# State-space chunks: decays from differences of prefix sums that every partition reads from memory, in place of matrix products

## The reference, cut to what matters

```python
def ssd_chunked(xs, dt, A, Bm, Cm):
    ...
    xd = (xs * dt[..., None]).reshape(b, c, CHUNK_3, H, P)
    a = (dt * A).reshape(b, c, CHUNK_3, H).transpose(0, 3, 1, 2)
    a_cs = jnp.cumsum(a, axis=-1)
    L_intra = jnp.exp(segsum(a))
    scores = jnp.einsum('bclhn,bcshn->bhcls', Ch, Bh) * L_intra
    y_diag = jnp.einsum('bhcls,bcshp->bclhp', scores, xd)
    ...
```

## Time and profile before

| | us |
|---|---|
| median of three runs (3662.11 to 3667.56) | 3666.65 |
| the profiled execution, its own time | 3663.11 |
| its span in the profile | 3661.3 |
| TensorE busy, and its share of the span | 3538.3, 97% |
| VectorE busy | 2080.5, 57% |
| ScalarE busy | 935.3, 26% |
| GpSimd busy | 1093.3, 30% |
| mean granted TensorE clock, as a share of full speed | 0.988 |

### The profile page before, as it was taken

How to read it: one execution, slowest core, us unless ns; L and a number is a source line. 1 busy time by engine, 2 the same in 40 slices (tenths; PEclk the granted TensorE clock), 3 DMA queues, 4 the chain that set the end, 5 groups by cost and what they waited for, 6 DMA issues and landing times. The chain is left out here.

```text
span 3661.3 us, 46083 instructions
## 1 busy us (share of the span) xinstructions
PE 3538.3 (97%) x18166; PEld 2876.8 (79%) x18166; DVE 2080.5 (57%) x2838; ACT 935.3 (26%) x1662; POOL 1093.3 (30%) x1069
## 2 busy tenths in 40 slices
PE   7999999999999999999999999799999999999998
PEld 5777776688888888788888888588878878787776
DVE  6464557524233236699945555644535697753564
ACT  4444445300000004311111100411221123652132
POOL 2221121233333333233332233033332234024332
PEclk9999999999999999999999999999999999999999
DMA  2010010212212111122221121221293224432211
GB/s 100 24 30 30 24 35 13 75 58 62 70 57 74 57 57 58 35 98 86 86 81 70 41 81 65 91 87 41 87 181 86 82 78 131 145 103 75 73 54 64
DMA packets 139240, 260.19 MB, mean 71 GB/s; under 512 B 45632, under 2 KB 87616, under 8 KB 136000
## 3 DMA queue, kind: packets, MB, share of 16 engines
q1 hardware_dynamic: 73360, 156.78, 14.7%
q10 hardware_dynamic: 65712, 101.10, 8.1%
HBM read 209.35 MB, written 46.14 MB: 70 GB/s over the span
## 5 line engine op out<-in xcount | busy, mean ns | idle before, releaser
L650 PE MATMUL bank<-xh,wh 128*128 128x512 f32 x3024 | 1192.8, 394 | 30.1 <-DVE xl L2107 12.1
L653 PE MATMUL bank<-xl,wh 128*128 128x512 f32 x3024 | 1183.1, 391 | 0.0
L654 PE MATMUL bank<-xh,wl 128*128 128x512 f32 x3024 | 1181.9, 391 | 0.0
L609 POOL CAST wh<-raw 128x512 fp32r<-128x512 f32 x528 | 345.7, 655 | 2364.4 <-PE bank L654 2202.5
L611 POOL TENSOR_TENSOR wl<-raw,wh 128x512 fp32r<-128x512 f32 x528 | 733.9, 1390 | 42.3
L650 PEld LDWEIGHTS bank<-xh,wh 128*128 128x128 f32 x3024 | 569.4, 188 | 168.0 <-issue 18.7
L654 PEld LDWEIGHTS bank<-xh,wl 128*128 128x128 f32 x3024 | 569.5, 188 | 122.3 <-issue 0.7
L653 PEld LDWEIGHTS bank<-xl,wh 128*128 128x128 f32 x3024 | 570.0, 188 | 118.0 <-issue 1.3
L2407 DVE SCALAR_TENSOR_TENSOR bank<-apad,cols,bank 128x512 f32<-128x512 f32 x406 | 267.9, 751 | 0.0
L2145 DVE TENSOR_TENSOR h<-bank,h 128x512 f32<-128x512 f32 x240 | 165.6, 691 | 145.5 <-PE bank L654 144.8
L2276 DVE TENSOR_TENSOR gt<-sa,bank 128x512 f32<-128x512 f32 x44 | 30.3, 688 | 347.8 <-PE bank L654 347.8
(11 more groups left out here) (339 smaller groups left out, 4876.9 us busy)
## 6 DMA issues: line engine op xcount, KB each, us to landing
raw<-in_wstream SPq DMA_DIRECT2D x264, 512.0 KB, 3.5
spills<-spill ACTq DMA_DIRECT2D x38, 512.0 KB, 2.9
rawm<-in_mod_w ACTq DMA_DIRECT2D x12, 1024.0 KB, 4.9
gate_spill<-gates ACTq DMA_DIRECT2D x16, 512.0 KB, 2.6
tabs<-in_rope ACTq DMA_DIRECT2D x4, 2048.0 KB, 8.9
f<-spills SPq DMA_DIRECT2D x8, 1024.0 KB, 5.6
h<-in_x ACTq DMA_DIRECT2D x4, 1024.0 KB, 11.8
tabs<-gate_spill ACTq DMA_DIRECT2D x4, 1024.0 KB, 7.4
```

The source lines that it names most:

```text
L609: nc.gpsimd.tensor_copy(wh[:, slot, k], raw[:, slot, k]).then_inc(S("panel_high"), 1)
L650: mm = nc.tensor.matmul(o, lh, rh, start=start, stop=False, skip_group_check=shared)
L653: nc.tensor.matmul(o, lh, rl, start=False, stop=False, skip_group_check=shared)
L654: return nc.tensor.matmul(o, ll, rh, start=False, stop=stop, skip_group_check=shared)
```

## The change

The prefix sums that `dec_sum` leaves in bank 3 are copied, negated, into `dtmp` (step on the partitions, chunk and head along the free dimension). TensorE transposes `dtmp` once (`cs_turn`), between the halves of the first `z_last` tile. ScalarE copies the transpose out with the sign turned back, and writes it to memory as 128 rows of 128 steps, one row per chunk and head (`cs_rows`, 64 KB). For each chunk one DMA on SP's queue reads the chunk's 16 rows, 8 KB, into every one of the 128 partitions (`csb`, 1 MB in all). ScalarE then forms |prefix(t) - prefix(s)| in 16 instructions of 128x128 (`Abs` with `dtmp` as a bias per partition) and exp(-x) in place in four of 128x512. The products with `after` and the operand `mt` are gone, and `csb` takes the room of `mt`. VectorE multiplies with the masked scores group by group, and `ssd_intra` waits group by group. The wait of `ssd_inter` on the decays is dropped, and `ssd_turn_x` gains one on `xt_ready`.

In SP's program the DMA of `csb` for chunk c stands ahead of that of `f`. For c = 0 it waits for the stored rows and for `pc_ready`, for later chunks until ScalarE has read the chunk before out of `csb`, which has one buffer.

```diff
@@ sync: chunk loop
                 for c in range(CHUNKS):
+                    if c:
+                        sp.wait_ge(S("lt_spans"), 4 * c)
+                    else:
+                        sp.wait_ge(S("cs_stored"), 16)
+                        sp.wait_ge(S("pc_ready"), KT)
+                    sp.dma_start(csb[:, :, :].rearrange("p h t -> p (h t)"),
+                                 cs_rows.rearrange("(c h) t -> c (h t)", c=CHUNKS)[c:c + 1].broadcast_to(
+                                     [P, SSD_HEADS * P])).then_inc(S("csb_in"), 16)
                     for m in range(2 if c == 0 else 0):
                         sp.wait_ge(S(f"spilled{m}"), 16 * 19)
@@ tensor
+                def cs_turn():
+                    pe.wait_ge(S("cs_kept"), 1)
+                    nc.tensor.transpose(banks[2][:, 0:P], dtmp[:, :, :].rearrange("p c h -> p (c h)"), M["ident"]
+                                        ).then_inc(S("dec_sum"), 1)
...
                 for m in range(2):
-                    tile_x(units("z_last") + 2 * m, panels("z_last") + m, between=lambda: s5_outputs(6 + m))
+                    def within_z():
+                        if m == 0:
+                            cs_turn()
+                        s5_outputs(6 + m)
+
+                    tile_x(units("z_last") + 2 * m, panels("z_last") + m, between=within_z)
...
             def ssd_turn_x(c):
                 pe.wait_ge(S(f"f_in{c % 2}"), (c // 2 + 1) * 16)
+                if c:
+                    pe.wait_ge(S("xt_ready"), c)
...
-            def ssd_decays(c):
-                pe.wait_ge(S("mt_ready"), c + 1)
-                for q in range(4):
...
-                    nc.tensor.matmul(banks[seg_banks[q]][:, :], M["after"],
-                                     mt[:, 4 * q:4 * q + 4, :].rearrange("p h t -> p (h t)"),
-                                     start=True, stop=True).then_inc(S("seg_done"), 1)
...
             def ssd_intra(c):
-                pe.wait_ge(S("w_masked"), c + 1)
                 for hd in range(SSD_HEADS):
+                    if hd % 4 == 0:
+                        pe.wait_ge(S("w_masked"), 4 * c + hd // 4 + 1)
...
             def ssd_inter(c):
-                pe.wait_ge(S("lt_ready"), 4 * c + 4)
...
-                ssd_decays(0)
...
-                        ssd_decays(c + 1)
@@ scalar
                     if e == DT_SOFT:
                         softplus()
+                act.wait_ge(S("dec_sum"), 1)
+                A(dtmp[:, :, :].rearrange("p c h -> p (c h)"), banks[3][:, 0:P], ACT.Copy, scale=-1.0
+                  ).then_inc(S("cs_kept"), 1)
                 for m in range(2):
...
                     if m == 0:
-                        act.wait_ge(S("pc_ready"), KT)
-                        for part in range(2):
-                            ssd_steps(0, part)
                         y_store(6)
+                        act.wait_ge(S("dec_sum"), 2)
+                        A(cs_turned, banks[2][:, 0:P], ACT.Copy, scale=-1.0).then_inc(S("cs_kept"), 1)
+                        act.wait_ge(S("cs_kept"), 2)
+                        act.dma_start(cs_rows[:, :], cs_turned).then_inc(S("cs_stored"), 16)
                 load_functions(EXP_AND_LN)
-                act.wait_ge(S("dec_sum"), 1)
@@ ssd_exp
-                for q in range(4):
-                    act.wait_ge(S("seg_done"), 4 * c + q + 1)
-                    A(lt[:, 4 * q:4 * q + 4, :], banks[seg_banks[q]][:, :].rearrange("p (h t) -> p h t", t=P),
-                      ACT.Exp).then_inc(S("lt_ready"), 1)
+                act.wait_ge(S("csb_in"), 16 * c + 16)
+                for hd in range(SSD_HEADS):
+                    mm = A(lt[:, hd, :], csb[:, hd, :], ACT.Abs, bias=dtmp[:, c, hd:hd + 1])
+                    if hd % 4 == 3:
+                        mm.then_inc(S("lt_spans"), 1)
+                for g in range(SSD_GROUPS):
+                    act.wait_ge(S("lt_spans"), 4 * c + g + 1)
+                    A(lt[:, 4 * g:4 * g + 4, :], lt[:, 4 * g:4 * g + 4, :], ACT.Exp, scale=-1.0
+                      ).then_inc(S("lt_ready"), 1)
...
-                for part in range(2):
-                    ssd_steps(1, part)
...
-                    if c + 2 < CHUNKS:
-                        ssd_steps(c + 2, 0)
                     ssd_root(c)
-                    if c + 2 < CHUNKS:
-                        ssd_steps(c + 2, 1)
@@ vector: ssd_weights
-                dve.wait_ge(S("lt_ready"), 4 * c + 4)
                 dve.wait_ge(S("sm_ready"), c + 1)
-                l4 = lt[:, :, :].rearrange("p (g h) t -> p g h t", g=SSD_GROUPS)
-                V.tensor_tensor(l4, l4, sm[:, :, :].unsqueeze(2).broadcast_to([P, SSD_GROUPS, 4, P]), ALU.mult
-                                ).then_inc(S("w_masked"), 1)
+                for g in range(SSD_GROUPS):
+                    dve.wait_ge(S("lt_ready"), 4 * c + g + 1)
+                    l4 = lt[:, 4 * g:4 * g + 4, :]
+                    V.tensor_tensor(l4, l4, sm[:, g, :].unsqueeze(1).broadcast_to([P, 4, P]), ALU.mult
+                                    ).then_inc(S("w_masked"), 1)
```

More of the change, by code:

```diff
@@ L418, in build @@
             xe = sb("xe", [P, D], F32, st)
-            mt = sb("mt", [P, SSD_HEADS, P], F32, st)
+            csb = sb("csb", [P, SSD_HEADS, P], F32, st)
             lt = sb("lt", [P, SSD_HEADS, P], F32, st)
@@ L443, in build @@
         y_spill = dram("y_spill", [D, S5_TAU, S5_BLOCKS])
+        cs_rows = dram("cs_rows", [P, P])
         h_spill = dram("h_spill", [P, KT, T])
@@ L446, in build @@
         block = ctx.enter_context(nc.Block())
-        seg_banks = [5, 0, 1, 5]
+        cs_turned = msum[:, 0:P]
         def settled(eng):
@@ L1773, in spill_tiles @@
                         act.dma_start(spills[n * 2 + (first + m)], spill[:, m, :]).then_inc(S(f"spilled{m}"), 16)
[L1775 to L1783, removed]
             if "s5_u" in run:
```

## The result

The changed kernel takes **3686.3 us** (median of 5 runs, 3683.2 to 3690.4), the kernel before 3665.7 beside it (5 runs, 3662.1 to 3667.6). The ratio is 1.0057, 95% interval 1.0046 to 1.0068: slower by 0.6%, and 3.3 us above the forecast of 3683. The profiled execution has a span of 3685.0 us against 3661.3.

What follows compares the result with a forecast made beforehand. The prediction took TensorE to bound the kernel before and a loop through ScalarE after. Its terms, 3.4 + 3.5 + 4.7 + 1.7 + 2 + 2.5 = 17.8 us on 3663.1, gave 3680.9, adjusted for scatter to 3683; range 3669 to 3702.

Steps and rivals of the forecast that it cites:

- Part 1: Chunk loop: TensorE loses 27.5 us of products and needs 13.60 us a chunk, a gain only where no other chain is longer.
- Part 2: Chunk loop: a loop through ScalarE's `Abs`, `exp` and square and back through TensorE takes 17.52 us against 17.04: +3.4 us.
- Part 3: Chunk loop: TensorE, idle 3.9 us a chunk, loses clock speed after waits: +3.5 us, between 0 and 12.
- Part 4: Transpose in `z_last`: waits for ScalarE's copy behind the DMA issues of `y_store(5)`, +4.7 us, and clock, +1.7: together 6.4.
- Part 5: Before chunk 0: the rows' store and read through memory make `f` land after TensorE is ready: +2 us.
- Part 6: Chunks 0 and 1: `dd` wait lengthens to 4.6 us, `f` of chunk 1 lands late: +2.5 us, from 0 to 4.5.
- the slow shared read: Rival: reading one 8 KB piece into 128 partitions takes 11.8 us, decisive above 7.4, giving 3723 us; chance 0.10.
- Only the start costs: Rival: ScalarE's loop comes to 17.1 us and the clock stays up, leaving 6.4 and a little more, 3671 to 3675; chance 0.14.
- TensorE as the pace: Rival: TensorE still sets the chunk loop's pace, so the kernel gets faster, 3654 or 3636 us; chance 0.06.

Runs made afterwards that it cites:

- e5_thin_products: The kernel before, with the `after` products of chunks 1 to 7 cut from 512 to 32 columns, other engines' work kept: 3663.6 us, ratio 0.9999.
- e6_spare_products: The changed kernel with four spare 128x512 products a chunk added on TensorE, 3.44 us a chunk: 3682.8 us, ratio 1.0047 to the kernel before.
- e1_copy_early: The changed kernel with ScalarE's copy of the prefix sums put ahead of the eight DMA issues of `y_store(5)`: 3684.3 us, ratio 1.0061 to the kernel before.
- the second execution: The profiled execution of the changed kernel run once more, unchanged; that run's median was 3690.9 us, ratio 1.0071 to the kernel before.
- e4_abs_slot: The changed kernel with the 16 `Abs` made in place in `csb`, one chunk ahead, where `mt` was made: 3686.4 us, ratio 1.0066 to the kernel before.
- e10_reorder: The changed kernel with copy, `f` and `dd` early, `h` after chunk 3, `Abs` in place a chunk ahead, VectorE and turns reordered: 3664.5 us, ratio 1.0002.

## Why the prediction was right, and where it was not

The sum was 17.8 us and the medians differ by 20.6. The direction and its reason were right; that the sizes lie so close is in part luck. In the profiled executions the stage lost 27.6 us, 9.8 more than the sum. Outside the stage 3.9 came back by chance, and the medians lie 3.1 closer together than the two profiled executions. By its parts:

- **Part 1** held, and more strongly than I wrote it: the 3.44 us are no gain where another chain is longer. `e5_thin_products` shows that this was so before the row read added anything. The Trainium skill's rule on the most contended engine ("Perfetto Trace Analysis", Identifying the Most-Contended Engine) named the right engine, but the second loop stood 0.35 us behind it.
- **Part 2** was right almost piece by piece: 17.56 us for 17.52. ScalarE's part came to 9.41 for 9.32 (16 `Abs` 4.66 for 4.68), TensorE's to 8.15 for 8.20. It cost 0.52 a chunk, 3.6 in seven (one of them is within the 8.8 of part 6).
- **Part 3**, clock and waits in the loop, was sized at 3.5 for the whole loop and measured 6.6 over six chunks in one profile and 3.8 in the other, inside its 0 to 12. `e6_spare_products` shows the cause.
- **Part 4** was right in its mechanism, and two errors in it nearly cancel: 6.8 us for 6.4 (5.5 in the second execution). The wait was 3.48 (4.4), and L784 began 4.0 later (4.7), as the queue issued its eight DMAs in 4.91 us and not in 5.80. The clock cost 2.8 (1.7): 1.8 in L784 and the rest in the matmuls behind it, as the granted clock was still 0.71 from 3094 to 3096 us. `e1_copy_early` shows the cause.
- **Part 5** was priced at 2 and cost nothing. The failed term is the way of the 64 KB store: I gave it 3.1 us to land, and SP issued `csb` at 3106.92, 1.58 after the store's issue at 3105.34. `csb` itself took 4.8 as forecast, and `f` was in place.
- **Part 6** is the step that failed. It gave chunks 0 and 1 2.5 us, 4.5 at most, and they cost 2.3 + 8.8 = 11.1 (1.0 + 9.1 in the second execution). The wrong term is the landing of `f` beside `h`. I took at worst `h`'s 14.4 us from the issue of `csb`, as if all three loads ended together. That is 3132.5 in the times of before, and 3138.1 in those of the change, where chunk 0 begins 5.6 us later. `csb` was issued when I said (3123.78), but `f` landed 5.0 us behind that worst case, at 3143.1, for two reasons. `h` took 16.6 us beside the row read instead of 14.4. And `f` didn't share with `h`: it came 2.9 us behind `csb`, which had itself landed only with `h`. TensorE wanted `f` at 3135.9. The other term is chunk 0. The wait for `dd`, 4.69, was as forecast (4.6), but the clock at half speed nearly doubled L1265 and lengthened L1281, where I had 1.7 as a possibility.
- The rest of the kernel was 2.7 us shorter, which no part had. One wait of 2.94 us for VectorE's `h`, the same in both, was followed by a granted clock of 0.52 in before (3513 to 3520 us) and of 1.00 after (3536 to 3543). It is chance: the same changed kernel run again took 416.0 there, as before did (415.9).

Of the rivals, the slow shared read fell: 4.8 us, and 7.4 was its point. "Only the start costs" was half right in size, as the starts are the larger part: 18 of the stage's 27.6 us. TensorE as the pace fell with `e6_spare_products`. I had sought the floor below ScalarE's loop in VectorE's busy time, 14.5; the path through it is 16.69, so even a ScalarE at 7.2 would not have paid for the starts; `e4_abs_slot` took the `Abs` out of its part and stayed at 3686.4.

## What to carry to other kernels

Before work is taken off the busiest engine, trace the next longest loop piece by piece, through every engine that it crosses: here it was 0.35 us behind, and the removal paid only once both were cut (17.04 to 14.1 us a chunk). A loop's length is that of its path, not the busy time of one engine in it. Reads in small packets on one queue were late here while a load in large packets ran on another: put such a load where nothing small is awaited, and order the small ones by who waits first.

## What the runs showed of the hardware

- A load in large packets on one queue holds back one in small packets on another, as the two move packet for packet. Beside 123 packets of `h` with 4.03 MB, the row read moved 127 packets with 1.04 MB (8 KB each); in `e10_reorder`, beside 91 packets of `h` with 2.98 MB, `f` moved 80 with 0.04 MB (512 bytes each). The row read landed in 16.4 us where it takes 4.8, and `f` behind it in 18.9 where it takes 7.6. The Trainium skill ("DMA: Bandwidth & Descriptors", Queues, rings and completion order) says that an engine takes turns between its queues packet by packet; these rows agree with it, for two sizes of packet on the queue that was held back.
- In the changed kernel the issue of a third load behind two of 1 MB lasted until the first had landed: 3.7 to 4.2 us in chunks 2 to 7, and 15.42 beside `h`, where SP's next issue came at 3140.11, right behind it.
- A read of 8 KB into all 128 partitions, 1 MB in all, lands in 4.65 to 4.94 us when no other load is in flight ahead of it on its queue (seven reads of the changed kernel), about as `rawm` does with 1 MB of its own (4.9).
- More work on TensorE made the loop no longer: 3.44 us of spare products a chunk, done in its waits, kept the granted clock at 1.00 where it was 0.94, and the six chunks took 105.4 us where they took 111.9 and 109.2.
